# Six of eight modulation vectors computed between the pieces of norm 1 and the first projections

## What is computed

```python
mod_ctx = (jax.nn.silu(c_ctx) @ w_mod[l] + b_mod[l])[None, None, :]
mod_lat = (jax.nn.silu(c) @ w_mod[l] + b_mod[l])[:, None, :]
...
shift1, scale1, gate1, shift2, scale2, gate2 = jnp.split(mod, 6, axis=-1)
h = rms_norm(x, lp["g_norm1"]) * (1 + scale1) + shift1
mixed, ctx_t = token_mixing(h, lp, lam_init, ctx)       # u = h @ w_in, four attention branches
x = x + gate1 * mixed
h = rms_norm(x, lp["g_norm2"]) * (1 + scale2) + shift2
x = x + gate2 * expert_choice_ffn(...)
```

## Time and profile before

| what | us |
|---|---|
| median of 3 runs (lowest, highest) | 2861.49 (2858.13, 2862.93) |
| the profiled execution, its span | 2852.66, 2850.6 |
| first matmul | 9.29 |
| first matmul of the D projection | 122.94 |
| E, end of the last `qm` | 200.67 |

### The profile page before, as it was taken

The page is one execution under the profiler, slowest core; times in us unless marked ns, Lnnn a source line. Parts: engine busy times, 40 slices in busy tenths (PEclk is TensorE's granted clock), DMA queues, the critical chain, the costliest instruction groups (busy, mean ns, idle before and its releaser), DMA issues.

```text
span 2850.6 us, 40449 instructions
## 1 busy us (share of the span) xinstructions
PE 2651.6 (93%) x13576; PEld 1831.1 (64%) x13576; DVE 1930.0 (68%) x2986; ACT 1628.5 (57%) x2399; POOL 466.2 (16%) x359
## 2 busy tenths in 40 slices
PE   7898999999999999999989899999999799999995
PEld 1486666767774666666658666676777366666663
DVE  7743566444357999999955356644535799999995
ACT  7635545444324777777743554444522477777774
POOL 1030002212301221121013000131231111112211
PEclk9899999999999999999999999999999899999997
DMA  9630112112447999999972111121234599999995
GB/s 369 243 93 30 34 38 71 48 46 66 162 173 281 379 381 379 379 378 376 387 241 80 43 34 38 46 74 38 74 128 178 205 376 376 381 377 385 379 381 185
DMA packets 191183, 593.74 MB, mean 208 GB/s; under 512 B 23628, under 2 KB 33674, under 8 KB 191054
## 3 DMA queue, kind: packets, MB, share of 16 engines
q1 hardware_dynamic: 171646, 527.68, 50.0%
q0 software_dynamic: 19408, 64.37, 7.7%
HBM read 566.73 MB, written 25.23 MB: 208 GB/s over the span
## 4 chain that ended last, share of the span: by engine, by line
PE 77%; DVE 9%; ACT 6%; issue 5%; DMA 3%; POOL 0%; ACTq 0%; SPq 0%; DVEq 0%; POOLq 0%
PE bank L530 22%; PE bank L532 20%; PE bank L531 20%; PE bank L941 4%; PE bank L969 3%; PE bank L956 2%; ACT high L1179 2%; DVE low L1554 1%; DMA ring<-in_w_mod 1%; DVE st L1863 1%; DMA U<-x_normed,idx_g 1%; PE bank L1090 1%; PE bank L795 1%; PE bank L725 1%; PE bank L1128 1%
## 5 line engine op out<-in xcount | busy, mean ns | idle before, releaser
L1179 ACT ACTIVATE high<-ring 128x1024 fp32r<-128x1024 f32 (+1 forms) x976 | 1023.4, 1052 | 393.0 <-PE bank L532 362.2
L1994 DVE TENSOR_TENSOR low<-ring,high 128x1024 fp32r<-128x1024 f32 x736 | 880.3, 1219 | 72.8 <-ACT high L1179 70.7
L530 PE MATMUL bank<-high,hT_high 128*128 128x512 f32 (+2 forms) x1280 | 516.5, 404 | 29.0 <-ACT sigr L1276 12.1
L531 PE MATMUL bank<-low,hT_high 128*128 128x512 f32 (+2 forms) x1280 | 485.6, 379 | 0.0
L532 PE MATMUL bank<-high,hT_low 128*128 128x512 f32 (+2 forms) x1280 | 484.8, 379 | 0.0
L530 PE MATMUL bank<-high,xeT_high 128*80 128x512 f32 x1056 | 419.0, 397 | 5.6 <-issue 3.5
L531 PE MATMUL bank<-low,xeT_high 128*80 128x512 f32 x1056 | 416.7, 395 | 0.0
L532 PE MATMUL bank<-high,xeT_low 128*80 128x512 f32 x1056 | 416.6, 395 | 0.0
L1554 DVE TENSOR_TENSOR low<-ring,high 128x1024 fp32r<-128x1024 f32 (+2 forms) x240 | 287.2, 1218 | 115.5 <-ACT high L1179 113.8
L530 PEld LDWEIGHTS bank<-high,hT_high 128*128 128x128 f32 x1280 | 242.6, 190 | 95.3 <-ACT sigr L1276 18.8
L1400 ACT ACTIVATE att<-bank,st 128x640 f32<-128x640 f32 (+3 forms) x200 | 136.3, 681 | 249.2 <-DVE st L1868 208.1
(11 more groups left out here) (261 smaller groups left out, 3177.3 us busy)
## 6 DMA issues: line engine op xcount, KB each, us to landing
ring<-in_w_e_gate SPq DMA_DIRECT2D x256, 512.0 KB, 6.2
ring<-in_w_e_up SPq DMA_DIRECT2D x256, 512.0 KB, 7.0
ring<-in_w_e_down SPq DMA_DIRECT2D x256, 512.0 KB, 6.4
ring<-in_w_mod SPq DMA_DIRECT2D x64, 512.0 KB, 6.5
ring<-in_w_gate SPq DMA_DIRECT2D x64, 512.0 KB, 4.2
ring<-in_w_in SPq DMA_DIRECT2D x24, 512.0 KB, 4.7
U<-in_w_mod SPq DMA_DIRECT2D x20, 512.0 KB, 5.1
ring<-in_w_branch SPq DMA_DIRECT2D x16, 512.0 KB, 4.4
```

Source lines behind the costliest of these rows:

```text
L530: nc.tensor.matmul(out, lhs[0], rhs_high, start=start, stop=False)
L531: nc.tensor.matmul(out, lhs[0], rhs_low, start=False, stop=False)
L1179: A(high[:, HSLOT[g], :, 0:w], ring[:, SLOT[g], :, 0:w], ACT.Copy).then_inc(high_done, 1)
L1994: V.tensor_tensor(low[:, SLOT[ahead], :, :], ring[:, SLOT[ahead], :, :], high[:, HSLOT[ahead], :, :].bitcast(F32), ALU.subtract).then_inc( ...
```

## The change

- A vector is made in two halves of 512 columns, 16 halves (`HALVES`), each from four chunks of 256 rows by 512 columns (512 KB as before). The order of `FIRST` is another: shift1 and scale1 of layer 0 first.
- Only the first four halves (`AHEAD`), 16 chunks, are made ahead through `ring`. The other 48 chunks (`N_MOD`) go through four raw buffers (`mod_raw`: three in `U`, one in `M`, later `att`) and three for the high parts. The low part overwrites the raw chunk.
- One list, `EARLY` (by `plan_early`), gives the order of layer 0's modulation chunks, norm pieces, projection pieces, tails, `ct` and `qm`; each engine walks through it. TensorE does chunk j at its place; ScalarE and VectorE make there the parts of chunk j + 3; SyncE fetches chunk j + 4 there, and waits at j = 0 for the first pair of broadcast rows (`gain_in[0]`).
- `modrow` and `modsum` alternate between two buffers; a tail writes bank 3 alone. `norm_turn` and `ct` of layer 0 use two banks, `qm` one.
- Three of the five token tiles are loaded after the first pair of broadcast rows, not at the start. The four later chunks of each projection and the tables and caches are fetched at places of `EARLY`, the tables at the first piece of D's third tile.
- POOL walks through 16 stores and bias rows. It waits for all of them before its rotary work on A.

```diff
+FIRST = [(0, 0), (0, 1), (0, 4), (1, 1), (1, 4), (0, 2), (0, 3), (0, 5)]
+HALVES = [(l, s, h) for l, s in FIRST for h in range(2)]
+AHEAD = 4
+CH_MOD = AHEAD * NQ_MOD
+N_MOD = (N_HALF - AHEAD) * NQ_MOD
+MOD_RAW, MOD_HIGH = 4, 3
+def plan_early():
+    out, j = [], 0
+    def mods(n):
+        nonlocal j
+        for _ in range(n):
+            out.append(("mod", j))
+            if j % NQ_MOD == 0 and j:
+                out.append(("tail", AHEAD + j // NQ_MOD - 1))
+            j += 1
+    mods(2)
+    out.append(("rms", 2))
+    mods(2)
+    out.extend([("rms", 3), ("rms", 4), ("stats", 0), ("turn", 0), ("stats", 1)])
+    for m in range(T):
+        for kq in range(NQ):
+            if kq == 1 and m + 1 < T:
+                out.append(("turn", m + 1))
+            out.append(("dense", ("W", "D"), m, kq))
+            if kq == 1 and m + 2 < T:
+                out.append(("stats", m + 2))
+            if kq < 3 or m == T - 1:
+                mods(1)
+    norm = [("square", m) for m in range(T)] + [("variance",)] + [("kpe", m) for m in range(TS)] + [("scaled", m) for m in range(T)]
+    for m in range(T):
+        for kq in range(NQ):
+            out.append(("dense", ("W", "Aq"), m, kq))
+            if kq % 2 or (m == T - 1 and kq == 0):
+                mods(1)
+            if norm:
+                out.append(norm.pop(0))
+    for m in range(T):
+        out.append(("ct", m))
...
+        for kq in range(NQ):
+            out.append(("dense", ("W", "Akv"), m, kq))
+            if kq < 3 or m < 2:
+                mods(1)
...
+            def mod_fill(j):
+                if j >= MOD_RAW:
+                    sp.wait_ge(mod_used, j - MOD_RAW + 1)
...
+                        if what == "mod" and x[0] + MOD_RAW < N_MOD:
+                            if x[0] == 0:
+                                sp.wait_ge(gain_in[0], 32)
+                            mod_fill(x[0] + MOD_RAW)
...
+                        if what == "dense" and x == [("W", "D"), 2, 0]:
                             sp.dma_start(rope[:, :, :], k_rope.rearrange("(m p) n -> p m n", p=P)).then_inc(table_in, 16)
...
                             small_loads()
...
+            def mod_chunk(j):
+                n, kq = AHEAD + j // NQ_MOD, j % NQ_MOD
+                pe.wait_ge(mod_low, j + 1)
+                if kq == 0 and n > AHEAD:
+                    pe.wait_ge(mod_row, n - 1)
+                mod_part(n, kq, mod_high_of(j), mod_low_of(j)).then_inc(mod_used, 1)
...
+            def mod_split(j):
+                act.wait_ge(mod_full[j % MOD_RAW], 16 * (j // MOD_RAW + 1))
+                if j >= MOD_HIGH:
+                    act.wait_ge(mod_used, j - MOD_HIGH + 1)
...
+                        if n == AHEAD - 1:
                             for b in range(2):
-                                pool.wait_ge(mod_out[b], 16)
-                            for g in (1, 0):
-                                mod_in(q1, g)
+                                pool.wait_ge(mod_out[b], 16 * AHEAD // 2)
+                            mod_in(q1, 1)
+                            for m in range(2, T):
+                                pool.dma_start(xt1[:, m, :], tok_in(l, m)).then_inc(x_in[m], 16)
+                            mod_in(q1, 0)
```

More of the change, by code:

```diff
@@ L657, in _ @@
                             small_loads()
+                        if what == "dense" and x[1] == T - 1:
+                            in_chunk(CHUNK0[x[0]] + x[2] + RING)
+                    n = CHUNK0["W", "Akv"] + NQ + RING
+                for kind, i in STREAM:
+                    if l == 0 and CHUNK0[kind, i] < n:
+                        continue
+                    if kind == "W":
+                        dense(w_in[l], *W_IN[i])
                         if l and i == "D":
@@ L1684, in _, with scaled @@
                     dve.wait_ge(kpe_ready, TS * l + m + 1)
[L1685 to L1687 removed]
+                def scaled(m):
+                    if m == 0:
+                        dve.wait_ge(c_sd, l + 1)
+                        then(V.reciprocal(r10, r10))
                     V.scalar_tensor_tensor(out=uD[:, m, 0:QR], in0=uD[:, m, 0:QR], scalar=r10[:, 2 * m:2 * m + 1],
```

526 lines of the change are left out of this document (322 added, 204 removed).

## The result

| | median us (lowest to highest, runs) | profiled execution, its span |
|---|---|---|
| before | 2860.69 (2857.21 to 2862.93, 6) | 2852.66, 2850.6 |
| changed | 2878.85 (2872.33 to 2883.82, 6) | 2874.3, 2872.5 |

A forecast was written before the change was run, and what follows sets the result against it. Transfers bound the opening, TensorE the projections. First D matmul at 62.5 plus 135.4 us (77.7 + 40.9 + 10.8 + 1.0 + 4 + 1) put E, the projections' end, at 197.9 against 200.67: 2.8 saved, median 2858.7, range 2848 to 2870.

The forecast's parts named there:

- the way to the first D matmul: Opening: bias row, store, pair, chunks 4 to 6, norm and turn in sequence put the first D matmul at 62.5 us.
- bias row: Opening, step 1: the fourth half's tail waits for its bias row, landing at 36.3 us; TensorE ready near 33.5.
- 2. store of half 3 landed: Opening: POOL issues the store behind tail and copy and waits until it has landed, at 40.2 us.
- 3. pair landed: Opening: the latent tokens' rows `M` and `oTr`, 512 KB each, take 4 and 1.3 us more, until 45.5.
- 4. chunk 6 landed: Opening: chunks 4 to 6, fetched after the pair, stand ahead of tile 0's norm; 1.5 + 3 x 2.55, until 54.7 us.
- 5. norm of tile 0 done: Before D: high part 0.95, low part 1.14, then norm and reciprocal 2.65 us, done at 59.4.
- The rival with a chance of 0.13: Projections: many short TensorE waits lower the clock; at 0.93, 10 us more than forecast, 2869; chance 0.13.
- Tables: D: 20 table and cache fetches delay chunk 14's fetch, stalling TensorE 4 us, bounds 2 and 6.
- rival of the late pair: D and Aq: late fetches hold back VectorE and ScalarE; small stalls cost 8 us instead of 1, 2865.7; chance 0.19.
- three chunks of lead: D and Aq: argument against the late pair, that VectorE and ScalarE work three chunks ahead of TensorE.
- terms of 0.93 a chunk and 0.9 a tail: First D matmul to E: 44 moved chunks add 40.9 us to TensorE's work, 12 tails 10.8 us.
- the forecast's own 58 to 66 us: Start of the first D matmul assumed for the forecast of 2858.7 us, own range 2853 to 2864; chance 0.48.

The follow-up runs named there:

- norm first: Changed kernel with ScalarE's and VectorE's norm pieces of tiles 0 and 1 ahead of the parts of modulation chunks 4 to 6; 2863.68 us, ratio 1.0004 to before.
- filler of 90: Changed kernel with 90 matmuls, whose result nobody reads, ahead of the turn of tile 0; 2875.08 us, ratio 1.0053 to before.
- two ahead: Changed kernel with ScalarE and VectorE making the parts of chunk j + 2 instead of j + 3; 2868.15 us, ratio 1.0025 to before.
- two profiles of before: The unedited kernel before, profiled twice; medians 2860.69 and, in the second, 2864.32 us, ratio 1.0001.
- tables spread: Changed kernel with the 20 table and cache fetches issued two at each modulation chunk from chunk 4 on; 2869.62 us, ratio 1.0031 to before.

## Why the prediction was wrong

Two steps failed. The larger is the clock: the sum had no term for it, and it cost 7.9 us between the first D matmul and E. The other is the way to the first D matmul, whose mechanism was right and whose terms were too small by 6.5 us together. Waits and work hold the remaining 4.5.

**The opening, step by step.** The 16 chunks' last tail started at 37.8 us (36.3 forecast). Its bias row landed at 37.7, as the last to come, but only by 0.1: TensorE and the evacuation were done at 37.6, where TensorE had been taken to be ready near 33.5.

| step of the prediction | forecast | measured |
|---|---|---|
| 2. store of half 3 landed | 40.2 | 42.3 |
| 3. pair landed | 45.5 | 48.8 |
| 4. chunk 6 landed | 54.7 | 59.4 |
| ScalarE begins its high part | 54.7 | 60.6 |
| 5. norm of tile 0 done | 59.4 | 65.6 |
| first D matmul | 62.5 | 69.0 |

The mechanism of step 4, the norm behind three chunks fetched only after the pair, was right, and norm first proved it. Its size failed in small parts. The store landed 2.1 us late, 1.6 of it from the tail and its copy. The pair took 6.5 us behind the store, not 5.3, and 1.1 of that is the issuing of the two rows, which had no term. Chunk 4 took 8.06 us to land, where 1.5 + 2.55 had been taken; it landed right behind the second pair (56.8 and 56.6 us). Chunks 5 and 6 then came 1.2 and 1.3 behind it, not 2.55 each, so that step 4 was 1.5 us too short in the end: the sharing was there, but all of it in front of the first chunk. ScalarE began chunk 6's high part 1.2 us after it had landed, held by a square-and-root piece and an evacuation. The last steps add 0.6. Together 6.5 us of the miss.

**From the first D matmul to E: 147.8 us, not 135.4.** The 12.4 us are:
- *The clock, 7.9 us.* The rival with a chance of 0.13. D's work is 51.58 us at 0.88 and 46.05 at 1.00 (filler of 90): 5.5 us. Aq's is 31.33 at 0.90 and 28.97 at 1.00 (two ahead): 2.4 us. The mean of the three stretches is 0.93, the value at which the rival had put its 10 us. This is the step that failed: the prediction said "clock at 1.00 but for the first microseconds of D", and its sum held nothing for those first microseconds, beyond what the 26.39 us of D before carry at their clock of 0.96, nor for what follows a wait. The first came to 9.3 us at the half level, 4.2 us of cost; what stands behind the waits in D and Aq is the other 3.7. The 4.2 are in part chance: of the profiled kernels that come to D as the changed one does, itself among them, four have 9.0 to 9.4 us of half level there and three 2.7 to 3.9. The argument used against the rival, that "with chunks in hand the opening ran at the full level from 31 us on", is a wrong reading of the trace of before. It holds up to about 77 us; from there to the first D matmul the clock was 0.76:

```profile
31.00:76.60 45.60, 40.94 (x150) 10.52 (x148) 41.65 (x40) 36.95 (x41) 5.64 (x11) 1.00 1.01 387
76.60:122.94 46.34, 37.28 (x108) 10.15 (x109) 37.03 (x40) 31.23 (x42) 4.53 (x9) 0.76 0.91 326
```

The rule cited there (the Trainium skill, "TensorE: Matmul & The Clock Gate", section "A second HAM failure mode: psum-queue depth-cycling") speaks of short idle moments between groups that make the clock swing, and the half-level matmuls behind the waits at 105.5 and 139.6 us agree with it. They are not the whole: the wait of 3.12 us in the filler of 90 left the clock at 1.00.
- *Waits, 7.2 us against 5.* Tables 3.3, inside the bounds of 2 to 6 around 4. In Aq 1.1 and 2.0 instead of 1, in Akv 0.8 instead of nothing. This is the rival of the late pair, 3.9 us where it had 8, by the mechanism that it gave: a fetch that lands late holds back ScalarE's evacuations, for which the tails wait. What spoke for it there, VectorE's load, matters for the last 2 us (two ahead). What spoke against it, "three chunks of lead", did not hold. The prediction compared a lead of "four chunks, 10 to 12 us, against 5 + 2.1"; but ScalarE asks for the chunk one place behind its fetch, 2.6 us later (Aq's 29 us of work for 11 chunks), so it met the landing each time, with evacuations queued behind it.
- *The work itself, 2.3 us.* D 46.05 for 45.9, Aq 28.97 for 27.9, Akv 57.66 for 56.6. The terms of 0.93 a chunk and 0.9 a tail were near.

**The sum.** 6.5 + 12.4 = 18.9 us later at E than forecast, of the 20.2 by which the median missed. From E to the end the changed kernel takes 2655.7 us, between the 2650.1 and 2660.1 of the two profiles of before. The rotary work on A was hidden, as said: it ends near 241 us, and its first reader, the turn of A's first heads, starts at 309.8.

**The forecast's shape.** A later start had no rival, only the forecast's own 58 to 66 us; clock and late pair were each a case of their own with the others at their forecast. All three came together, clock and late pair in part for one reason: a queue that stands at a fresh transfer makes the wait, and in Aq the lower clock went with it. The range was built from single cases and ended 8.9 us short.

## What to carry to other kernels

When work is moved into gaps, price not only the wait that it brings but the clock behind it: here 4.2 us went to slower matmuls behind the idle stretch ahead of D, and 3.7 more behind waits of 7.2 us. Read the clock of the old kernel in short stretches before using it as an argument; a mean of 0.86 hid one of 0.76. In an engine's queue place work that waits for a fresh transfer behind all that is ready, and check at each place how long ago its fetch went out; asking for a chunk two places ahead instead of three was 8 us faster at E, 2.7 of it in the start and 2.9 in Aq. Spread a run of small fetches over a loop instead of issuing it in one piece, and keep it away from a small store that somebody waits for.

## What the runs showed of the hardware that wasn't expected

- After an idle stretch the matmuls stayed at the half level for lengths that differ between nearly equal kernels: from D's first matmul 9.3 us in the changed kernel, 2.7 us with the tables spread. 11.5 us of steady matmuls that ended 6.1 us ahead of the next piece left no trace in its pace; behind 17.1 us that reached to it the pace was the full one. Each is one execution.
- The landing time of a small store depends on what is beside it: one of 4 KB took 2.46 us in the changed kernel and 6.20 with the tables' transfers beside it.
- A fetch of 512 KB issued 2.8 us behind the last of seven transfers of another queue landed 0.2 us behind the last of them, after 8.06 us; the next two landed 1.2 and 1.3 us behind it.
